# A streaming encoder step on one core: where the first tile's convolution hides, and where its LayerNorms take their sums

## The reference, cut to what matters

```
proj = x @ w_in                       # q (512), k (128), v (128), u (1024)
attn = window_attention(rope(q), rope(k), v, sinks)      # chunks of 64, window 128
c    = u[:512] * sigmoid(u[512:])                        # GLU
c    = depthwise_conv(c, 31 taps) + bias
c    = silu(layer_norm(c))                               # "cln", 512 features
h    = layer_norm(2**0.25 * x + concat(attn, c) @ w_out) # "ln1", 1024 features
up   = depthwise_conv(h @ w_up, 3 taps)                  # 5632 columns
f    = (silu(up[:2816]) * up[2816:]) @ w_down
ple  = sigmoid(h @ w_pg + b_pg) * (p @ w_pe)
y    = layer_norm(2**0.25 * h + f + ple)                 # "ln2", 1024 features
```

## Time and profile before

| | us |
|---|---|
| median of three runs | 2574.2 (2570.93 to 2574.41) |
| the profiled execution: its own time | 2572.75 |
| its span, from the first to the last instruction | 2570.9 |
| PE busy in it | 2384.2 (93%) |
| DVE busy | 1530.2 (60%) |
| ACT busy | 1276.0 (50%) |
| POOL busy | 1490.0 (58%) |
| mean granted TensorE clock | 0.962 |

### The profile page before, as it was taken

How to read it: one execution, slowest core, us unless ns; L and a number is a source line. 1 busy time by engine, 2 the same in 40 slices (tenths; PEclk the granted TensorE clock), 3 DMA queues, 4 the chain that set the end, 5 groups by cost and what they waited for, 6 DMA issues and landing times.

```text
span 2570.9 us, 38014 instructions
## 1 busy us (share of the span) xinstructions
PE 2384.2 (93%) x15013; PEld 2344.2 (91%) x15013; DVE 1530.2 (60%) x2366; ACT 1276.0 (50%) x2060; POOL 1490.0 (58%) x648
## 2 busy tenths in 40 slices
PE   7578998989999989999998999999899999969995
PEld 7477898989999989999998999999889999969995
DVE  5835886376666447666645766662666665354433
ACT  4236656446553535645353564444455435345653
POOL 7245676665555565555565655556565554746763
PEclk9788999989999999999999999999999999989998
DMA  6133454633333353333344433334343333524442
GB/s 229 64 100 108 146 165 136 204 114 132 122 117 129 122 171 122 131 113 125 125 142 141 148 114 114 128 114 158 127 156 116 123 123 104 176 90 165 165 148 87
DMA packets 119041, 341.50 MB, mean 133 GB/s; under 512 B 15312, under 2 KB 43600, under 8 KB 118864
## 3 DMA queue, kind: packets, MB, share of 16 engines
q1 hardware_dynamic: 93360, 308.70, 36.1%
q10 hardware_dynamic: 25504, 30.37, 3.8%
HBM read 330.12 MB, written 8.99 MB: 132 GB/s over the span
## 4 chain that ended last, share of the span: by engine, by line
PE 83%; DVE 10%; ACT 4%; issue 1%; POOL 1%; DMA 1%; ACTq 0%; DVEq 0%
PE ps L481 27%; PE ps L483 26%; PE ps L482 26%; DVE sq L1057 4%; PE ps L548 1%; DVE res L997 1%; POOL w_lo L433 1%; PE ps L520 1%; ACT w_hi L575 1%; PE ps L529 1%; PE ps L539 1%; DMA w_raw<-in_panels 1%; ACT h_raw L781 1%; DVE a_lo L869 1%; ACT sq L768 0%
## 5 line engine op out<-in xcount | busy, mean ns | idle before, releaser
L433 POOL TENSOR_TENSOR w_lo<-w_raw,w_hi 128x1024 fp32r<-128x1024 f32 (+1 forms) x636 | 1489.0, 2349 | 1042.7 <-ACT w_hi L575 1042.3
L575 ACT CAST w_hi<-w_raw 128x1024 fp32r<-128x1024 f32 (+1 forms) x636 | 622.2, 981 | 566.8 <-PE ps L483 460.1
L481 PE MATMUL ps<-h_hi,w_hi 128*128 128x386 f32 (+5 forms) x2496 | 821.5, 329 | 22.8 <-POOL w_lo L433 20.9
L482 PE MATMUL ps<-h_lo,w_hi 128*128 128x386 f32 (+5 forms) x2496 | 812.0, 325 | 0.0
L483 PE MATMUL ps<-h_hi,w_lo 128*128 128x386 f32 (+5 forms) x2496 | 811.9, 325 | 0.0
L481 PEld LDWEIGHTS ps<-h_hi,w_hi 128*128 128x128 f32 x2496 | 478.5, 192 | 31.0 <-POOL w_lo L433 22.1
L482 PEld LDWEIGHTS ps<-h_lo,w_hi 128*128 128x128 f32 x2496 | 479.2, 192 | 1.8 <-issue 0.6
L483 PEld LDWEIGHTS ps<-h_hi,w_lo 128*128 128x128 f32 x2496 | 479.0, 192 | 0.0
L481 PE MATMUL ps<-f_hi,w_hi 128*128 128x384 f32 (+2 forms) x1264 | 415.8, 329 | 2.5 <-POOL w_lo L433 1.7
L482 PE MATMUL ps<-f_lo,w_hi 128*128 128x384 f32 (+2 forms) x1264 | 408.8, 323 | 0.0
L483 PE MATMUL ps<-f_hi,w_lo 128*128 128x384 f32 (+2 forms) x1264 | 408.4, 323 | 0.0
(11 more groups left out here) (118 smaller groups left out, 2064.7 us busy)
## 6 DMA issues: line engine op xcount, KB each, us to landing
w_raw<-in_panels SPq DMA_DIRECT2D x540, 512.0 KB, 3.3
w_raw<-in_panels SPq DMA_DIRECT2D x48, 384.0 KB, 3.1
w_raw<-in_panels SPq DMA_DIRECT2D x48, 128.0 KB, 2.3
xres<-in_xT ACTq DMA_DIRECT2D x32, 192.0 KB, 2.9
out_yT<-res ACTq DMA_DIRECT2D x4, 1536.0 KB, 5.6
a_raw<-in_xT ACTq DMA_DIRECT2D x6, 768.0 KB, 6.0
out_yT<-res ACTq DMA_DIRECT2D x2, 1024.0 KB, 4.9
x_raw<-in_xT ACTq DMA_DIRECT2D x1, 1536.0 KB, 11.4
```

Source lines behind the costliest of these rows:

```text
L433: pool.tensor_tensor(w_lo[:, n % WS, 0:w], w_raw[:, n % RS, 0:w], w_hi[:, n % WS, 0:w].bitcast(F32), ALU.subtract).then_inc(w_lo_done, 1)
L481: pe.matmul(out, w_hi[:, sl, c], hi, start=k == 0, stop=False)
L482: pe.matmul(out, w_hi[:, sl, c], lo, start=False, stop=False)
L575: act.copy(w_hi[:, n % WS, 0:w], w_raw[:, n % RS, 0:w]).then_inc(w_hi_done, 1)
```

## The change

In words:

- **The first tile's cover.** The eight GLU groups and v of the second tile now run before `out` of the first tile, beside its attention and its remaining 71 taps (9 and 8 taps by turns). The k and the four q groups (`LATE`) move behind `out`, as the fill beside `ln1` of the first tile. Their rotation on DVE, which was part of taking the group away, becomes a stage of its own (`rope`) that is placed by hand among the steps of that LayerNorm.
- **Places of the LayerNorm steps.** In tiles 1 to 4 the sum of squares of `ln1` goes from place 5 to 6, `var` and `root` from 6 to 9, `scale` from 7 to 10, `affine` from 9 to 12, `lo` from 10 to 13; all steps of `ln2` go two places later. The low part of the next tile's input on DVE (`x_low`) goes from place 3 to 5. In the last tile the steps of both LayerNorms are placed anew.
- **Sums on PE.** For four LayerNorms (`DIRECT`) the pairwise sums on DVE are gone, both the one of the values and the one of the squares; PE instead multiplies all eight (four) blocks with the matrix of 1/1024 and adds them in PSUM.
- **The halo** of the low part is copied in place at the first `out` group, and the copy behind the low part of `ln1` is gone.

```diff
+LATE = [IN_K] + list(range(IN_Q, IN_Q + HB))
...
         if g == 5:
             stage("x_split", 1)
+            stage("x_low", 1)
+
     side = {0: [("vt", 0)], 1: [("scores", 0, 0)], 3: [("divide", 0, 0)], 4: [("turn", 0, 0)],
-            5: [("mixed", 0, 0), ("scores", 0, 1)]}
-    for n, g in enumerate(KVQ):
+            5: [("mixed", 0, 0)], 6: [("scores", 0, 1)], 8: [("divide", 0, 1)]}
+    for n, g in enumerate(GLU + [IN_V]):
         for what in side.get(n, ()):
             stage(*what)
         stage("in", 1, g)
-        first_taps((3, 7, 4, 4, 4, 4)[n])
-    first_taps(10)
-    stage("divide", 0, 1)
+        first_taps(9 if n % 2 == 0 else 8)
     stage("turn", 0, 1)
-    first_taps(8)
+    first_taps(3)
     stage("mixed", 0, 1)
...
-        fill = [("d", i - 1, 2, m) for m in range(KB)] if i else [("in", 1, g) for g in GLU]
+        fill = [("d", i - 1, 2, m) for m in range(KB)] if i else [("in", 1, g) for g in LATE]
...
         if 1 <= i < LAST:
-            one = {2: ("mean", "centre"), 3: ("square",), 5: ("sqtree",), 6: ("var", "root"), 7: ("scale",),
-                   9: ("affine",), 10: ("lo",)}
-            two = {9: ("tree",), 11: ("mean", "centre"), 12: ("square",), 14: ("sqtree",), 16: ("var", "root"),
-                   17: ("scale",), 19: ("affine",)}
+            one = {2: ("mean", "centre"), 3: ("square",), 6: ("sqtree",), 9: ("var", "root"), 10: ("scale",),
+                   12: ("affine",), 13: ("lo",)}
+            two = {11: ("tree",), 13: ("mean", "centre"), 14: ("square",), 16: ("sqtree",), 18: ("var", "root"),
+                   19: ("scale",), 21: ("affine",)}
+        elif i:
+            one = {0: ("mean", "centre", "square"), 3: ("var", "root", "scale", "affine", "lo")}
+            two = {}
         else:
-            one = {1: ("mean", "centre"), 2: ("square",), 3: ("sqtree",), 4: ("var", "root"), 5: ("scale",),
-                   6: ("affine",), 7: ("lo",)}
+            one = {0: ("mean", "centre", "square"), 2: ("var", "root", "scale"), 4: ("affine",), 5: ("lo",)}
             two = {}
+        if i == 0:
+            one = {0: ("mean", "centre", "square", 0), 2: ("var", "root", 1, "scale"), 4: (2, 3, "affine", "lo", 4)}
         for n, g in enumerate(fill):
             stage(*g)
             for name in one.get(n, ()):
+                if name in (0, 1, 2, 3, 4):
+                    stage("rope", 1, LATE[name])
+                    continue
                 stage(name, "ln1", i)
...
-            if 1 <= i < LAST and n == 3:
-                stage("x_split", i + 1)
-        late = {0: ("tree",), 1: ("mean", "centre", "square"), 2: ("sqtree",), 3: ("var", "root", "scale"), 4: ("affine",)}
+            if 1 <= i < LAST and n in (3, 5):
+                stage("x_split" if n == 3 else "x_low", i + 1)
+        late = {0: ("tree",), 2: ("mean", "centre", "square"), 3: ("sqtree",), 5: ("var", "root", "scale"), 6: ("affine",)}
...
+DIRECT = (("cln", 0), ("ln1", 0), ("ln1", LAST), ("ln2", LAST))
...
+            def sum_of_blocks(name, t, done, b, ones):
+                z, hi, lo, nb, w = ln_of(name, t)
+                n = LN_NO[name, t]
+                if done is mean_done:
...
+                    if name == "cln":
+                        pe.wait_ge(conv_done, 1)
+                        pe.wait_ge(att_done, unit_no(t, UNITS[t]))
+                    elif name == "ln1":
+                        pe.wait_ge(z_done, (t + 1) * KB)
+                    else:
+                        pe.wait_ge(down_done, (t + 1) * 3 * KB)
+                else:
+                    pe.wait_ge(sq_done, n + 1)
+                    z = sq[:, :, 0:w]
+                for k in range(nb):
+                    mm = pe.matmul(ps[:, b, 0:w], ones[:], z[:, k, :], start=k == 0, stop=k == nb - 1)
+                mm.then_inc(done, 1)
...
             act.wait_ge(zero_set, 1)
+            act.copy(h_lo[:, :, 0:FHALO], h_keep[:])
             act.copy(h_hi[:, :, 0:FHALO], h_keep[:]).then_inc(h_halo, 1)
...
-                elif k >= IN_K and k != IN_V:
+                elif k >= IN_K and k != IN_V and (t != 1 or now):
...
-                    dve.tensor_copy(h_keep[:], h_lo[:, :, before:before + FHALO].bitcast(F32))
+                    own.step(dve.tensor_copy(h_lo[:, :, 0:FHALO], h_lo[:, :, before:before + FHALO]))
+                    own.wait()
                     dve.tensor_copy(h_hi[:, :, 0:FHALO], h_hi[:, :, before:before + FHALO]).then_inc(h_halo, 1)
...
-                ins = dve.tensor_tensor(lo, z, hi.bitcast(F32), ALU.subtract)
-                if name == "cln":
-                    ins.then_inc(mix_lo, 1)
-                    return
-                own.step(ins)
-                own.wait()
-                dve.tensor_copy(h_lo[:, :, 0:FHALO], h_keep[:]).then_inc(h_ready, 1)
+                dve.tensor_tensor(lo, z, hi.bitcast(F32), ALU.subtract).then_inc(mix_lo if name == "cln" else h_ready, 1)
...
+                elif what == "rope":
+                    take_in(("in", *e[1:]), True)
...
-                elif what == "x_split":
+                elif what == "x_low":
                     split_x(e[1])
```

More of the change, by code:

```diff
@@ L210 @@
 assert len(NUM) == GROUPS == NT * PANELS
+SUM_NO = {e: n for n, e in enumerate([e for e in LN_NO if e not in DIRECT])}
 def panel_of(e):
@@ L323, in build @@
     gate_done, glu_done, qk_done, v_done = (sem(n) for n in ("gate_done", "glu_done", "qk_done", "v_done"))
-    conv_in, conv_read, halo_done = sem("conv_in"), sem("conv_read"), sem("halo_done")
+    conv_in, conv_read, conv_done, halo_done = sem("conv_in"), sem("conv_read"), sem("conv_done"), sem("halo_done")
     z_done, down_done, sig_done, ple_done, ple_added = (
@@ L546, in mean @@
                 ones = mean4 if name == "cln" else mean8
-                pe.wait_ge(arrived, LN_NO[name, t] + 1)
+                if (name, t) in DIRECT:
+                    sum_of_blocks(name, t, done, b, ones)
+                    return
+                pe.wait_ge(arrived, SUM_NO[name, t] + 1)
                 pe.matmul(ps[:, b, 0:WIDTH[t]], ones[:], sq[:, 0, 0:WIDTH[t]], start=True, stop=True).then_inc(done, 1)
+            def sum_of_blocks(name, t, done, b, ones):
+                z, hi, lo, nb, w = ln_of(name, t)
+                n = LN_NO[name, t]
+                if done is mean_done:
+                    if n:
+                        pe.wait_ge(scaled, n)
+                    if name == "cln":
[11 more added lines that the diff above has]
+                mm.then_inc(done, 1)
             for e in PLAN:
@@ L871, in split_x, with take_in @@
                 ins.then_inc(x_lo, 1)
-            def take_in(e):
+            def take_in(e, now=False):
                 _, t, k = e
@@ L1018, in convolved @@
                 for tok, col, cnt in prompt_and_sample(t, 0, G_SMP - HALO):
-                    own.step(dve.tensor_tensor(a_raw[1][:, c, tok:tok + cnt], odd[:, col:col + cnt], even[:, col:col + cnt],
-                                               ALU.add))
+                    ins = dve.tensor_tensor(a_raw[1][:, c, tok:tok + cnt], odd[:, col:col + cnt], even[:, col:col + cnt], ALU.add)
+                    if t == 0 and c == HB - 1:
+                        ins.then_inc(conv_done, 1)
+                    else:
+                        own.step(ins)
             def maxima(t, u):
```

## The result

| | before | changed |
|---|---|---|
| median of four runs each, one chip | 2574.1 us | 2542.4 us (2541.2 to 2546.4) |
| ratio, with its 95% interval | | 0.988 (0.9865 to 0.990) |
| the profiled execution: its own time / span | 2572.75 / 2570.9 | 2546.35 / 2544.5 |

The kernel is 31.6 us faster where 56 were forecast; 2542.4 is just above the range.

What follows compares the result with a forecast made beforehand. PE, busy 93% of the span, was taken as the bound. 2572.75 - 9.5 - 33 - 10.4 - 7.5 + 3.3 = 2515.6, so 2517 as median; forecast 2518 us, 8-in-10 range 2499 to 2542.

Steps and rivals of the forecast that it cites:

- Tile 0, `out` 3.5 us earlier: First tile: `out` starts 3.5 us earlier, from 6 us through the new cover less 2.5 for `cln` on PE.
- two softmax units at 1.7 + 1.7: Tile 0's DVE work after the mask: two softmax units at 1.7 us each, within some 40 us.
- `conv_add`, queued behind that low part on DVE, done at 126: Tile 0: `conv_add`, behind the low part of attention, ends at 126 us where it had ended at 132.0.
- Rival 4: The cover doesn't cover: tile 0's DVE queue ends last, tile 0 and `late` give nothing; 2535 us, chance 0.10.
- The price of `cln` on PE: Tile 0: two sums of 8 passes at 0.43 us each on PE make it 2.5 us worse together.
- Fills: Tiles 1 to 4: new LayerNorm places gain 11, 7.2, 7.2 and 7.5 us, 33 together, with a shorter wait at place 18.
- rival 1: `ln2`'s wait replaces `ln1`'s: tiles 1 to 4 each wait 6 to 9 us at place 18; 2541 us, chance 0.18.
- Tile 5, `ln1`: Last tile: sums on PE start `u` 8.2 us sooner, plus 2.2 of clock, 10.4 us gained.
- The end: Tail without fill: the two sums on PE cost 0.4 and 3 us more, 3.3 us lost.
- `late`: `ln2` of tile 4 among tile 5's `u` groups: later slots leave 11.5 us lost of 19, 7.5 us gained.
- Some 17 us better without it: Without DVE's contention with POOL, a sum ends 4 us sooner, `ln2`'s new wait vanishes, total some 17 us better.
- rival 3: The float32 sums don't stream: a pass costs 0.6 to 1.0 us; 2596 us at 1.0, chance 0.03.

Runs made afterwards that it cites:

- the repeat: The same changed kernel, unaltered, measured on another chip: 2538.3 us, ratio 0.987 to the kernel before, which took 2572.0 there.
- experiment 3: The changed kernel with `conv_add` placed ahead of the attention's split in tile 0: 2534.9 us, ratio 0.9856.
- Experiment 9: The changed kernel with POOL splitting only 128 of up to 1024 columns of each weight panel, other engines' instructions unchanged: 2466.1 us, ratio 0.9587.
- experiment 5: The changed kernel with the sums of `cln` in tile 0 and of the last tile's `ln2` back on DVE: 2536.5 us.
- experiment 2: The changed kernel with, in tiles 1 to 4, `lo` of `ln1` at place 14 and `ln2`'s sum of squares at 15: 2521.9 us, ratio 0.9805.
- Experiments 1 and 8: The changed kernel: 1 with the former places of `late`, 2542.1 us; 8 without seven of eight `affine` instructions of tile 4's `ln2`, 2535.3 us.
- experiment 4: The changed kernel with `ln2` of tile 4, among tile 5's `u` groups, also summed on PE: 2529.2 us, ratio 0.9835.

## Why the prediction came out as it did, point by point

- **Tile 0, `out` 3.5 us earlier: wrong, 3.3 later (2.0 in the repeat).** The step that failed is "two softmax units at 1.7 + 1.7" and with it "`conv_add`, queued behind that low part on DVE, done at 126". The second division took 5.4 us beside POOL, and `conv_add` was done at 132.7; 3.7 of the 6.7 us are that division, 1.8 the slower products behind it, and 1.2 had come together before it, which was not taken apart. The queue I had named myself; experiment 3 gives 3.4 us back by lifting it. Experiment 9 gives 17.3 by lifting POOL, but 9.4 of them at an earlier place, PE's first wait for the mask (12.5 to 3.1), which the forecast took as given. Before, the division met an idle POOL and took 1.7 us; it was the new cover, with its weights to split, that made it dear. Rival 4 had this half right: PE waited 1.6 and 5.1 us for the two divisions, where 2 and 1 were forecast. The price of `cln` on PE was 2.8 in experiment 5 for 2.5 forecast; the forecast's own terms, 8 x 0.43 against 1.15 + 1.22 twice, make only 2.1, and the passes cost 0.47. The stretch behind `out` was right (6.3 for 6.2).
- **Fills: the mechanism was right, the size off.** Tile 1 gained 10.8 for 11. In tiles 2 to 4 the wait went from place 6 to place 18, as said, and it was 3.7, 3.7 and 5.2 us (1 to 4 and, for tile 4, 5.4 forecast). Three terms make the difference in tile 2 (93.7 instead of 89.3). The floor is 85.8 and not 84.6, 1.2. Waits were 3.7 + 1.0 where I took 2.7, 2.0. What is left, the clock above all, is 3.2 where I took 2.0, 1.2; in the repeat, at a clock of 1.00, it is 0.7. The sum took 9.66 where I used, since each of its three additions came up behind a split, and at the first one POOL was 0.05 us ahead. Of rival 1's condition (k's rotation beside POOL, a sum of 8.6 or more) the second half came true and the first did not (the rotation's product with two SBUF inputs took 0.55 us), and its price, 6 to 9 us, did not come.
- **What I had not seen in the fills** is that `centre` needs nothing of `lo`. I wrote that it stands "on the same queue" and took it as given; experiment 2 shows that this order and the place of the sum, taken together, were worth 16.3 us.
- **Tile 5, `ln1`: right**, 10.5 for 10.4. **The end: right**, 3.4 lost for 3.3; 16 passes took 4.14 us at full and 7.03 at the lower clock, where I had 4.3 and 8.
- **`late`: wrong, 4.2 lost instead of 7.5 gained.** The failed step is "I count 1 + 7 of wait and 3.5 of clock". The two sums' waits were 1.6 + 4.5, less than I counted. But a third wait came, of 7.0 at the first `d` group, with 2.4 of clock behind it. I had followed the LayerNorm up to its second sum and not the `affine` that I moved two slots towards the `d` groups. Each `u` group costs ACT about 2.2 us of PE's 3.3, so by an estimate from these rows the 4.9 us of `affine` alone need some 4.5 groups to be worked off, and after the move there are three. Experiments 1 and 8 show both halves: the places mostly carry the wait along, and ACT's 4.3 us make 4.2 of it at its new place. The other 2.8 us of it were not taken apart; just ahead of `affine` ACT had stood 3.2 us for DVE, which was at `scale`.
- **The sum.** On the profiled executions 57.1 us were forecast and 26.4 came: 6.8 + 12.6 + 11.7 = 31.1 of error, with the rest within 0.4. The median lies 3.9 below the profiled execution. Of the signs named beforehand, the waits at place 18, the first `u` product (213.6) and the end (31.7) came as said; tile 2's fill (87 to 91 forecast, 93.7 and in the repeat 91.2) and the first `out` product (141 to 147 forecast, 150.9) did not.
- **Contention.** The estimate of 3.5 us for a free sum was right (3.75 in experiment 9; the means of its three forms, over all sums, are 1.85, 1.06 and 0.60). "Some 17 us better without it" was far too small; the fills of tiles 2 to 4 alone give 20.2 against the repeat. I priced it only where a wait was already on the page, and not at the divisions of tile 0.

## What to carry to other kernels

A step moved in an in-order list has to be followed to its last instruction, and past it to the next consumer of that engine's backlog: a wait that disappears at one slot often stands at the last slot before a hard dependence. Look at each queue for an instruction that waits for another engine with ready work behind it: experiments 2 and 3 reordered queues in this way and gave 20 of the 64 us here, more than moving any sum. But follow the ready work to what it feeds: by the rows of tile 2 the early `centre` alone would have gained nothing, since the sum stood behind a second wait. And count a DVE operation with two SBUF inputs beside a busy GpSimd as its own time plus up to one whole GpSimd instruction, for each instruction of a chain (not always: `lo` in tile 2 was under way 1.0 us before POOL's split began, and took 3.36 us with the full and with the light POOL). As for moving a sum to PE, it gained among the `u` groups, where PE stayed busy through it (experiment 4), and lost where PE had stood still before it (experiment 5).

## What the runs showed of the hardware that I had not expected

- An addition of eight elements took 2.06 us and a product 3.08 while POOL was at its splits of 2.4 us; before, with POOL idle, they took 0.16 and 1.23. What is added hardly depends on the size of the DVE operation, but on the phase: the same three additions took 7.52, 8.05, 8.62 and 9.66 us. The Trainium skill (GPSIMD Engine Reference, 8. Key points) names the contention; the price in this kernel is from these rows.
- The same program with the same wait of 3.7 us kept its full clock in one execution and lost it in another: fill of tile 2, 91.2 us at 1.00 in the repeat, 93.7 at 0.96 in the first profile. The two passes of the sum behind the wait took 0.91 and 1.65 us together. Row of the repeat:

```profile
913.70:1004.90 91.20, 86.55 (x489) 84.55 (x488) 71.55 (x51) 44.66 (x47) 63.01 (x22) 1.00 0.41 141
```

  These two ran on different chips, but experiments 3 and 5 show the same on one: 91.3 us at 1.00 and 93.8 at 0.96, behind the same wait. The fills of tiles 2 and 3 make 5.3 of the 9.3 us by which the profiled spans of the changed kernel and the repeat differ, so a wait of 3.7 us cost 2.5 more here or nothing.
- A float32 pass (one of the two records that each float32 matmul leaves in the trace) cost 0.26 us at 290 columns and full clock, 0.33 at 384, and 0.44 to 0.47 at the lower clock (290 and 256): PE streams them, and rival 3 had no ground.
